# Where the residual of the second half joins, and which chunks carry no late row, in a hybrid attention and PEER block

## The chip, the cores and the metric

The kernel runs on one core of a Trainium2 chip. The metric is the device time of one execution in microseconds (us). Engines: PE (TensorE), ACT (ScalarE), DVE (VectorE), POOL (GpSimd), SP (SyncE, which here only issues DMAs). A core has 16 DMA engines, which all queues share.

## The reference, cut to what matters

The block mixes two attentions and then a PEER layer over 256 tokens of width 2048, all in fp32. Everything before the PEER layer is the same in both kernels. What the change touches is the end:

```python
    def chunk(args):                      # peer(): 128 experts for each token
        xi, ei, gi = args
        u = expert_down[ei]
        a = jax.nn.gelu(jnp.einsum('cd,ced->ce', xi, u)).astype(jnp.float32)
        w = (a * gi).astype(xi.dtype)
        return jnp.einsum('ce,ced->cd', w, expert_up[ei])
...
        x = x + peer(rms_norm(x, norm_ffn_gain[l]), ...)
    return rms_norm(x, norm_final_gain)
```

`expert_up` has 16384 rows of 2048 floats, 128 MB. Each token needs 128 of them.

## The kernel before

**Two ways to form the sum over experts.** The 256 tokens are two halves of 128. For half 0, and for the first 64 tokens of half 1, the weights of a token are spread into a dense row over all 16384 experts, and PE multiplies them with the whole table. The table is read in 128 chunks of 128 experts, 1024 KB each (`u_raw`, four buffers, issued by SP at L672; chunk i is requested once PE has finished chunk i-4). Half 0 accumulates in PSUM banks 4 to 7 ("a"), the 64 tokens of half 1 in banks 0 to 3 ("b").

For the last 64 tokens of half 1 there is no dense path. Each token sits in two partitions, so that 128 partitions times 64 slots hold its experts. POOL gathers one row per partition (`late_rows`, 1 MB a gather, L1375). First come 63 gathers of `expert_down`, each reduced on DVE to a column of dot products (`late_dot`), then 64 gathers of `expert_up`, which DVE multiplies by the weight and adds into `late_sum` (`late_add`, L2454 to L2459). These are 127 late operations. They use six buffers; a gather is requested when the operation that last used its buffer is done, and POOL issues its gathers in order. Buffer 4 lies where the weights of chunks 0 to 15 were, and buffer 5 where those of chunks 16 to 31 were, so their first gathers wait for those chunks.

**One chunk.** Seven of eight chunks are split in a high and a low part: ACT rounds `u_raw` to `u_hi` (L1835) and the weights to `c_hi` and `c_b`; DVE forms `c_lo` and the low half of `c_b` (`c_low`), then `u_lo` (L2439), and then does the late operation of that chunk; PE does 12 matmuls with `u_hi` and 8 with `u_lo`. Each eighth chunk (i % 8 = 7) is "whole": PE uses it in fp32 and DVE has only the late operation.

**Which chunk carries a late operation.**

```python
        late_chunks = [i for i in range(1, NKEYS) if i % LATE_SKIP]
...
            for n_, j in enumerate(range(len(late_chunks), LATE_OPS)):
                if n_ == FINAL_0_AFTER:
                    final_0()
                late_op(j)
            final_1()
```

With `LATE_SKIP` = 24, chunks 24, 48, 72, 96 and 120 carry none; 122 of the 127 operations lie beside a chunk, and five lie behind the last one: three, then `final_0` (the output of half 0 from PSUM), then two, of which the last is cut in four pieces of 512 columns.

**The end.** ACT copies banks 0 to 3 to `b_out` (L1894) and takes the sum of squares of half 0 (L1711) and its root (L1713). Behind the last chunk PE adds into each bank c, for half 1: the residual (a matmul with the identity, all 128 rows), the fold of `b_out` (rows 0 to 63), and, as each piece of `late_sum` is ready, its fold (rows 64 to 127). ACT and DVE then norm half 1 bank by bank (`final_stats_1`, `final_1`), and SP stores it. SP also requests `final_row`, the gain of the last norm, 1024 KB, right behind the request of chunk 124.

Of the kernel before, what the change touches and what calls it, by code (L numbers as in the profile page):

```python
# [24 lines left out]
ALU = mybir.AluOpType  # L25
# [3 lines left out]
P = 128  # L29
# [125 lines left out]
IDLE = 1  # L155
WHOLE = 8
POOL_FROM = 3
LATE_SKIP = 24
FINAL_0_AFTER = 3
PRE = 1  # L160
QUARTER = D // 4
BT = 4
# [1 line left out]
PAIRS = P // 2  # L164
# [9 lines left out]
def build(nc, x, norm_mix_gain, w_in, nsa_gate_bias, fox_forget_bias, merge_gate_bias, k_cmp_pos, k_cmp_w1,  # L174
          k_cmp_w2, v_cmp_pos, v_cmp_w1, v_cmp_w2, w_up_nsa, w_up_fox, w_out, norm_ffn_gain, peer_w_query,
          peer_sub_keys_1, peer_sub_keys_2, peer_expert_down, peer_expert_up, norm_final_gain, consts, out):
    with ExitStack() as ctx:
        def sem(name):
            return ctx.enter_context(nc.semaphore(name))
# [4 lines left out]
        def at(name, shape, kb, dt=F32):  # L184
            n = int(np.prod(shape[1:])) * 4
            assert base + kb * 1024 + n <= nc.sbuf_usable_end, name
            return nc.alloc_sbuf_tensor_at(name, shape, dt, offset=int(base + kb * 1024))
# [21 lines left out]
        def const(name, parts=P):  # L209
            lo, hi = CT[name]  # L210
            return ct[0:parts, lo:hi]

        ident = const("ident")
# [22 lines left out]
        xres = at("xres", [P, HALVES, D], 138)  # L236
# [66 lines left out]
        u_hi = at("u_hi", [P, 2, D], 178, F32R)  # L303
# [5 lines left out]
        late_sum = at("late_sum", [P, D], 90)  # L309
        b_out = at("b_out", [P, D], 98)  # L310
        pair_sum = at("pair_sum", [P, PAIRS], 8)
        late_rows = [at(f"late_rows{r}", [P, D], kb) for r, kb in enumerate(LATE_AT)]
# [43 lines left out]
        psum = ctx.enter_context(nc.psum_tensor("psum", [P, 8, 512], F32))  # L356
# [120 lines left out]
        u_hi_used = sem("u_hi_used")  # L477
# [4 lines left out]
        pair_ps = sem("pair_ps")  # L482
# [65 lines left out]
        for d in range(len(ring_slots) + PRE):  # L548
            r = order[d] if d < len(order) else ring[(d - len(order)) % RING]
            if d >= LAST_SIX:  # L550
                r = (1, 7, 6, 2, 0, 3)[(d - LAST_SIX) % 6]
# [4 lines left out]
        LATE_OPS = 2 * LATE - PRE  # L556
        late_chunks = [i for i in range(1, NKEYS) if i % LATE_SKIP]

# [4 lines left out]
        def last_down(r):  # L563

            return max([d for d in range(len(down_slot)) if down_slot[d] == r and r < 4], default=NG * GS - 1)
# [3 lines left out]
        for j in range(LATE_OPS):  # L569
            free = [r for r in range(len(LATE_AT)) if LATE_FREE[r] <= late_step(j)]  # L570
            r = min(free, key=lambda r: last_op.get(r, last_down(r) - NG * GS))
# [115 lines left out]
        def _(pe):  # L687
            def mm(*a, **k):
                return nc.tensor.matmul(*a, skip_group_check=True, **k)  # L689
# [486 lines left out]
            for b in range(NBX):  # L1176
# [6 lines left out]
                if b == XRES_AT:  # L1183
                    pe.wait_ge(numT_done, 2)
                    pe.wait_ge(wT_done, 2)
                    for c in range(4):
                        last = mm(psum[:, 4 + c, :], ident, xres[:, 0, 512 * c:512 * c + 512], start=True, stop=False)
# [13 lines left out]
            def col(c):  # L1201
                return slice(512 * c, 512 * c + 512)
# [5 lines left out]
                    last = mm(psum[:, 4 + c, :], c_lo[:, q % 2, :], u_hi[:, q % 2, col(c)], start=False, stop=False)  # L1208
                return last

            def high_b(q, first=False):

                both = c_b[:, q % 2].rearrange("p x t -> p (x t)")
                for c in range(4):
                    last = mm(psum[:, c, :], both, u_hi[:, q % 2, col(c)], start=first, stop=False)
                return last

            def low_a(q, r):

                for c in range(4):  # L1220
                    last = mm(psum[:, 4 + c, :], c_hi[:, q % 2, :], u_lo[r][:, col(c)], start=False, stop=False)
                return last

            def low_b(q, r):

                both = c_b[:, q % 2].rearrange("p x t -> p (x t)")
                for c in range(4):
                    last = mm(psum[:, c, :], both, u_lo[r][:, col(c)], start=False, stop=False)
                last.then_inc(chunk_used, 1)

            def split_up(m, q, r):

                pe.wait_ge(u_hi_done, m + 1)
                pe.wait_ge(c_lo_done, m + 2)
                high_a(q)
                high_b(q).then_inc(u_hi_used, 1)
                pe.wait_ge(u_lo_done, m + 1)
                low_a(q, r)
                low_b(q, r)
# [36 lines left out]
            pe.wait_ge(u_lo_done, 1)  # L1276
            low_a(0, 0)
            pe.wait_ge(W_out, NBX + NB1)
            pe.wait_ge(c_lo_done, 2)
            high_b(0, first=True).then_inc(u_hi_used, 1)  # L1280
            low_b(0, 0)
            sixteen(0, first=1)
            with pe.Fori(1, NKEYS // 16 - 1) as i:
# [7 lines left out]
            pe.wait_ge(tables_done, 2)  # L1291
            for c in range(4):
                pe.wait_ge(b_copied, c + 1)
                mm(psum[:, c, :], ident, xres[:, 1, col(c)], start=True, stop=False)
                mm(psum[0:PAIRS, c, :], pair_sum[:], b_out[:, col(c)], start=False, stop=True)
            for c in range(4):
                pe.wait_ge(late_used, LATE_OPS + c)
                mm(psum[PAIRS:P, c, :], pair_sum[:], late_sum[:, col(c)], start=False, stop=True).then_inc(pair_ps, 1)


        @block.gpsimd
# [134 lines left out]
        def _(act):  # L1436
# [278 lines left out]
            def final_stats_1():  # L1715
                i = 2 * HALVES + 1
                for c in range(4):
                    cs = slice(512 * c, 512 * c + 512)
                    act.wait_ge(pair_ps, c + 1)
                    A(xn[:, 1, cs], psum[:, c, :], ACT.Square, accum_out=ss_end[:, c:c + 1]).then_inc(part_sums, 1)  # L1720
                act.wait_ge(ms_done, 2)
                A(rms[:, i:i + 1], ss[:, i:i + 1], ACT.Sqrt, bias=eps[:, 0:1], scale=1.0 / D).then_inc(squares, 1)
                act.wait_ge(x2_done, 1)
                A(xn[:, 1, OUT_COLS[0]], xres[:, 1, OUT_COLS[0]], ACT.Copy, scale=rstd[:, i:i + 1]).then_inc(x2_done, 1)
# [168 lines left out]
            for c in range(4):  # L1893
                nc.scalar.copy(b_out[:, 512 * c:512 * c + 512], psum[:, c, :]).then_inc(b_copied, 1)  # L1894
            final_stats_0()
            final_stats_1()


        @block.vector
        def _(dve):  # L1900
            V = nc.vector
            tt, ts, stt = V.tensor_tensor, V.tensor_scalar, V.scalar_tensor_tensor
# [543 lines left out]
            def late_add(j):  # L2446
                r, slot = late_slot[j], DENSE[1] + j - (LATE - PRE)
                w = gw[1].rearrange("p h s -> p (h s)")[:, slot:slot + 1]
                dve.wait_ge(late_in[r], 16 * late_turn[j])
                dve.wait_ge(late_used, j)  # L2450
                if j == LATE_OPS - 1:
                    for c in range(4):
                        cs = slice(512 * c, 512 * c + 512)
                        stt(late_sum[:, cs], late_rows[r][:, cs], w, late_sum[:, cs], ALU.mult, ALU.add).then_inc(late_used, 1)  # L2454
                    return
                if j == LATE - PRE:
                    ins = ts(late_sum[:], late_rows[r][:], w, None, ALU.mult)
                else:
                    ins = stt(late_sum[:], late_rows[r][:], w, late_sum[:], ALU.mult, ALU.add)  # L2459
                ins.then_inc(late_used, 1)  # L2460
# [35 lines left out]
            def late_op(j):  # L2496
                if j < LATE - PRE:
                    late_dot(j)
                else:
                    late_add(j)  # L2500
                if j == LATE_A - PRE:
                    late_inner(0, LATE_A)
                if j == LATE_A - PRE + 3:
                    late_weights(1, 0, LATE_A)
                if j == LATE - PRE:
                    late_inner(LATE_A, LATE)
                if j == LATE - PRE + 3:
                    late_weights(2, LATE_A, LATE)

            def final_0():  # L2510
                i = 2 * HALVES
                dve.wait_ge(squares, 3)
                seq(V.reciprocal(rstd[:, i:i + 1], rms[:, i:i + 1]))
                settle()
                dve.wait_ge(row_loaded, 16)
                x2 = psum[:, 4:8, :].rearrange("p k n -> p (k n)")
                for cs in OUT_COLS:
                    stt(xn[:, 0, cs], x2[:, cs], rstd[:, i:i + 1], final_row[:, cs], ALU.mult, ALU.mult).then_inc(y_done, 1)
# [93 lines left out]
# [3 lines that stand above are left out]
# [28 lines left out]
```

## Time and profile before

| what | value |
|---|---|
| median of three runs | 1964.7 us (1962.78 to 1968.36) |
| the profiled execution, its own time | 1965.54 us |
| its span, first to last instruction | 1963.7 us |
| mean granted PE clock | 0.975 of full |
| busy share PE, DVE, ACT, POOL | 93%, 76%, 44%, 30% |
| the stretch with the chunks | about 1316 to 1945 us |

A row of the timeline gives the start in us from the span's start, the duration in us, engine, line, operation, output<-inputs, and in brackets how long the engine idled before it and what ended that. PE matmuls are in fp32 or, with `u_hi` and `u_lo`, in a rounded form that needs one pass; one fp32 matmul shows as two. "DMA" in the column of an issue is the time from request to landing.

### The profile page before, as it was taken

The numbers are of one execution on the slowest core, as the hardware profiler recorded it, in microseconds if no ns is written. First come the engines' busy times: TensorE is split into PE (matmuls) and PEld (weight loads), VectorE is DVE, ScalarE is ACT, GpSimd is POOL, SyncE is SP. The second block draws the span as 40 slices with busy tenths as digits, with TensorE's granted clock in tenths as the row PEclk, the third lists the DMA queues.
The fourth block names the chain that finished last, engine by engine and source line by source line (L and its number), as shares of the span: only waits on it lengthen the run. The fifth ranks groups of instructions, "written<-read, shape, count | busy, mean of one in ns | idle before, by whom it ended". The sixth has DMA issues, their size and how long they took to land.

```text
span 1963.7 us, 26424 instructions
## 1 busy us (share of the span) xinstructions
PE 1824.8 (93%) x10535; PEld 1507.1 (77%) x10535; DVE 1500.9 (76%) x2000; ACT 858.6 (44%) x1262; POOL 584.5 (30%) x371
## 2 busy tenths in 40 slices
PE   8999999999999999879989757679999999999997
PEld 7979987888899879878888735467767776777674
DVE  5454447544455457899999999979989898998888
ACT  4343336444433343223333278974444434443443
POOL 1302300000000002646567678742333122222422
PEclk9999999999999999989999988989999999999999
DMA  7864550465556645899999999979999999999995
GB/s 259 291 228 148 174 169 22 129 192 186 187 183 225 237 140 171 338 426 402 401 426 426 420 382 425 404 317 398 427 427 427 427 427 427 428 428 427 426 427 230
DMA packets 142676, 620.25 MB, mean 316 GB/s; under 512 B 9680, under 2 KB 20192, under 8 KB 84464
## 3 DMA queue, kind: packets, MB, share of 16 engines
q0 software_dynamic: 46352, 336.11, 41.2%
q1 hardware_dynamic: 93712, 280.05, 38.3%
q10 hardware_dynamic: 2512, 2.75, 0.4%
q8 instruction: 64, 1.05, 0.2%
q14 instruction: 36, 0.29, 0.0%
HBM read 616.77 MB, written 2.10 MB: 315 GB/s over the span
## 4 chain that ended last, share of the span: by engine, by line
PE 58%; DVE 19%; DMA 9%; ACT 7%; issue 6%; POOL 1%; DVEq 0%; ACTq 0%; POOLq 0%
PE psum L689 57%; DMA u_raw<-in_peer_expert_up_dram 8%; DVE down_rows L2310 7%; DVE late_sum L2459 2%; ACT oh L1779 1%; ACT oh L1766 1%; ACT oh L1764 1%; DMA late_rows<-in_peer_expert_down_dram,eidx 1%; DVE w_lo L1950 1%; DMA down_rows<-in_peer_expert_down_dram,eidx 1%; DVE u_lo L2439 1%; DVE late_rows L2310 1%; ACT w_hi L1472 1%; ACT u_hi L1835 1%; DVE onehot L2266 1%
## 5 line engine op out<-in xcount | busy, mean ns | idle before, releaser
L1950 DVE TENSOR_TENSOR w_lo<-raw,w_hi 128x2048 fp32r<-128x2048 f32 x124 | 291.5, 2350 | 334.2 <-ACT w_hi L1472 334.1
L1472 ACT CAST w_hi<-raw 128x2048 fp32r<-128x2048 f32 x124 | 236.4, 1907 | 400.2 <-PE psum L689 400.2
L689 PE MATMUL psum<-act_both,w_hi 128*128 128x256 f32 (+1 forms) x1664 | 389.0, 319 | 4.4 <-DVE w_lo L1950 4.4
L1835 ACT CAST u_hi<-u_raw 128x2048 fp32r<-128x2048 f32 x112 | 214.3, 1913 | 356.2 <-DMA u_raw<-in_peer_expert_up_dram 351.9
L1375 POOL DMA_INDIRECT down_rows<-in_peer_expert_down_dram,eidx x155 | 280.8, 1812 | 121.1 <-issue 44.7
L689 PE MATMUL psum<-act_both,w_lo 128*128 128x256 f32 x1088 | 305.7, 281 | 0.0
L689 PEld LDWEIGHTS psum<-act_both,w_hi 128*128 128x128 f32 x1664 | 277.4, 192 | 28.0 <-issue 3.0
L2439 DVE TENSOR_TENSOR u_lo<-u_raw,u_hi 128x2048 fp32r<-128x2048 f32 x112 | 256.7, 2292 | 0.0
L689 PEld LDWEIGHTS psum<-act_both,w_lo 128*128 128x128 f32 x1088 | 207.7, 191 | 0.0
L2310 DVE CUSTOM_DVE_ANT_0 down_rows<-down_rows,xn 128x2048 f32<-128x2048 f32 x91 | 205.5, 2288 | 0.9 <-DVE ind L2221 0.4
L689 PE MATMUL psum<-w_hi,act_both 128*128 128x512 f32 x640 | 202.1, 394 | 0.2 <-DVE w_lo L1950 0.2
L689 PE MATMUL psum<-u_hi,c_hi 128*128 128x512 f32 x448 | 185.2, 413 | 9.7 <-DVE c_b L2468 6.7
L689 PE MATMUL psum<-xT,rT 128*128 128x128 f32 x1216 | 167.4, 288 | 25.0 <-DVE dots L2338 17.8
L689 PEld LDWEIGHTS psum<-xT,rT 128*128 128x128 f32 x1216 | 153.7, 199 | 33.7 <-issue 16.8
L689 PE MATMUL psum<-u_hi,c_lo 128*128 128x512 f32 x448 | 176.3, 393 | 0.0
L1800 ACT COPY rT<-psum 128x512 f32<-128x512 f32 x152 | 85.6, 588 | 200.1 <-PE psum L1055 200.1
L1375 POOL DMA_INDIRECT late_rows<-in_peer_expert_up_dram,eidx x64 | 92.3, 1442 | 242.8 <-DVE late_sum L2459 212.5
L1372 POOL TENSOR_TENSOR xn<-xn,ffn_row 128x2048 f32<-128x2048 f32 x2 | 11.3, 5654 | 496.2 <-PE psum L707 496.2
L2310 DVE CUSTOM_DVE_ANT_0 late_rows<-late_rows,xn 128x2048 f32<-128x2048 f32 x63 | 143.6, 2286 | 9.0 <-DMA late_rows<-in_peer_expert_down_dram,eidx 8.8
L1375 POOL DMA_INDIRECT late_rows<-in_peer_expert_down_dram,eidx x63 | 85.5, 1357 | 217.4 <-DVE keep L2310 178.7
L2459 DVE SCALAR_TENSOR_TENSOR late_sum<-late_rows,gw,late_sum 128x2048 f32<-128x2048 f32 x62 | 145.5, 2347 | 1.2
L2310 DVE CUSTOM_DVE_ANT_0 down_rows<-down_rows,x_b 128x2048 f32<-128x2048 f32 x64 | 142.7, 2289 | 0.1
(342 smaller groups left out, 3175.7 us busy)
## 6 DMA issues: line engine op xcount, KB each, us to landing
u_raw<-in_peer_expert_up_dram SPq DMA_DIRECT2D x128, 1024.0 KB, 11.8
raw<-in_w_in_dram SPq DMA_DIRECT2D x76, 1024.0 KB, 5.0
raw<-in_w_out_dram SPq DMA_DIRECT2D x16, 1024.0 KB, 4.9
raw<-in_peer_w_query_dram SPq DMA_DIRECT2D x16, 1024.0 KB, 5.0
raw<-in_w_up_nsa_dram SPq DMA_DIRECT2D x8, 1024.0 KB, 5.0
raw<-in_w_up_fox_dram SPq DMA_DIRECT2D x8, 1024.0 KB, 5.0
cmp_w<-in_k_cmp_w_dram SPq DMA_DIRECT2D x4, 1024.0 KB, 10.7
cmp_w<-in_v_cmp_w_dram SPq DMA_DIRECT2D x4, 1024.0 KB, 10.6
```

The source lines that it names most:

```text
L689: return nc.tensor.matmul(*a, skip_group_check=True, **k)
L1375: nc.gpsimd.indirect_dma_start(rows[:], None, table, bass.IndirectOffsetOnAxis(ap=eidx[:, half, slot:slot + 1], axis=0)).then_inc(landed, 16)
L1472: nc.scalar.copy(w_hi[:, p % 2], raw[:, p]).then_inc(hi_done, 1)
L1764: A(both, psum[:, 0:2, :], ACT.Abs).then_inc(dist_done, 1)
L1766: A(both, both, ACT.Relu, bias=1.0, scale=-1.0).then_inc(rows_done, 1)
L1779: ins = A(oh[:, 1, par, q, :], oh[:, 1, par, q, :], ACT.Copy, scale=w[:, q:q + 1])
L1800: nc.scalar.copy(dst.rearrange("p k t -> p (k t)"), psum[:, r % 2, :]).then_inc(rT_done, 1)
L1835: nc.scalar.copy(u_hi[:, m % 2, :], u_raw[i % 4][:]).then_inc(u_hi_done, 1)
L1950: tt(w_lo[:, p % 2], raw[:, p], f32(w_hi[:, p % 2]), ALU.subtract).then_inc(lo_done, 1)
L2310: return V.tensor_tensor_reduce(out=rows[:], in0=rows[:], in1=x_, scale=1.0, scalar=0.0, op0=ALU.mult, op1=ALU.add, accum_out=out)
L2439: tt(u_lo[i % 4][:], u_raw[i % 4][:], f32(u_hi[:, m % 2, :]), ALU.subtract).then_inc(u_lo_done, 1)
L2459: ins = stt(late_sum[:], late_rows[r][:], w, late_sum[:], ALU.mult, ALU.add)
```

## The change

Four edits. (1) The residual of tokens 0 to 63 of half 1 goes into banks 0 to 3 at chunk 0: four matmuls with 64 rows of the identity, ahead of the first use of those banks, and the four residual matmuls behind the last chunk go away. (2) The residual of tokens 64 to 127 goes into `late_sum` with the first weighted row: an operation over 128 partitions becomes two over 64 each. (3) `LATE_SKIP` 24 becomes 32: chunks 32, 64 and 96 carry no late operation, 124 of 127 lie beside a chunk and, counted in the code, three instead of five behind the last one. (4) `FINAL_0_AFTER` 3 becomes 2: two of the three come before `final_0`, the cut one behind it. In the final matmuls, rows 0 to 63 and 64 to 127 each get a start of their own, and the count that ACT waits for is shifted by four.

```diff
-LATE_SKIP = 24
-FINAL_0_AFTER = 3
+LATE_SKIP = 32
+FINAL_0_AFTER = 2
...
             low_a(0, 0)
             pe.wait_ge(W_out, NBX + NB1)
+            for c in range(4):
+                mm(psum[:, c, :], ident[0:PAIRS, :], xres[0:PAIRS, 1, col(c)], start=True, stop=False)
             pe.wait_ge(c_lo_done, 2)
-            high_b(0, first=True).then_inc(u_hi_used, 1)
+            high_b(0).then_inc(u_hi_used, 1)
...
             for c in range(4):
                 pe.wait_ge(b_copied, c + 1)
-                mm(psum[:, c, :], ident, xres[:, 1, col(c)], start=True, stop=False)
-                mm(psum[0:PAIRS, c, :], pair_sum[:], b_out[:, col(c)], start=False, stop=True)
+                mm(psum[0:PAIRS, c, :], pair_sum[:], b_out[:, col(c)], start=True, stop=True).then_inc(pair_ps, 1)
             for c in range(4):
                 pe.wait_ge(late_used, LATE_OPS + c)
-                mm(psum[PAIRS:P, c, :], pair_sum[:], late_sum[:, col(c)], start=False, stop=True).then_inc(pair_ps, 1)
+                mm(psum[PAIRS:P, c, :], pair_sum[:], late_sum[:, col(c)], start=True, stop=True).then_inc(pair_ps, 1)
...
-                    act.wait_ge(pair_ps, c + 1)
+                    act.wait_ge(pair_ps, 4 + c + 1)
...
                 if j == LATE - PRE:
-                    ins = ts(late_sum[:], late_rows[r][:], w, None, ALU.mult)
+                    ts(late_sum[0:PAIRS], late_rows[r][0:PAIRS], w[0:PAIRS], None, ALU.mult)
+                    ins = stt(late_sum[PAIRS:P], late_rows[r][PAIRS:P], w[PAIRS:P], xres[PAIRS:P, 1, :], ALU.mult, ALU.add)
```

## Rows read from the trace of the kernel before

**Rows 1.** The page, busy time of each engine

```profile
PE 1824.8 (93%) x10535; PEld 1507.1 (77%) x10535; DVE 1500.9 (76%) x2000; ACT 858.6 (44%) x1262; POOL 584.5 (30%) x371
```

**Rows 2.** Busy time by stretch: PE, PEld, DVE, ACT, POOL, clock, DMA share, GB/s

```profile
1314.00:1322.00 8.00, 7.98 (x46) 6.71 (x45) 6.14 (x12) 6.39 (x9) 1.75 (x2) 1.00 0.01 2
1324.00:1342.00 18.00, 18.00 (x79) 14.45 (x78) 18.00 (x21) 9.32 (x14) 3.84 (x4) 1.00 0.93 350
1342.00:1900.00 558.00, 552.21 (x2232) 397.17 (x2231) 510.18 (x479) 228.40 (x328) 154.03 (x113) 1.00 1.01 427
```

**Rows 3.** The chain that ended last, 1900 us to the end

```profile
1909.98 15.32 DMA u_raw<-in_peer_expert_up_dram
...
1952.87 3.66 PE psum L689 x8
...
1958.33 1.15 ACT xn L1724
```

**Rows 4.** Timeline of ACT, chunks 122 to 125

```profile
1907.19 1.92 ACT L1835 CAST u_hi<-u_raw 128x2048 fp32r<-128x2048 f32 x1 [2.66 <-DMA u_raw<-in_peer_expert_up_dram]
...
1912.09 1.92 ACT L1835 CAST u_hi<-u_raw 128x2048 fp32r<-128x2048 f32 x1 [2.64 <-DMA u_raw<-in_peer_expert_up_dram]
...
1915.16 1.92 ACT L1835 CAST u_hi<-u_raw 128x2048 fp32r<-128x2048 f32 x1 [0.82 <-DMA u_raw<-in_peer_expert_up_dram]
...
1925.33 1.90 ACT L1835 CAST u_hi<-u_raw 128x2048 fp32r<-128x2048 f32 x1 [7.91 <-DMA u_raw<-in_peer_expert_up_dram]
```

**Rows 5.** Timeline of POOL, the gathers' requests around chunks 120 and 121

```profile
1898.32 0.94 POOL L1375 DMA_INDIRECT late_rows<-in_peer_expert_up_dram,eidx  x1 [0.30 <-issue]
1909.72 0.99 POOL L1375 DMA_INDIRECT late_rows<-in_peer_expert_up_dram,eidx  x1 [10.47 <-DVE late_sum L2459]
```

**Rows 6.** DMA requests in 1904 to 1907 us: size, us to landing

```profile
final_row<-in_norm_final_gain_dram SPq DMA_DIRECT2D x1, 1024.0 KB, 14.1
```

**Rows 7.** Timeline of POOL, the gathers around the first use of buffer 5

```profile
1443.95 0.98 POOL L1375 DMA_INDIRECT late_rows<-in_peer_expert_down_dram,eidx  x1 [4.01 <-DVE keep L2310]
1459.77 2.24 POOL L1375 DMA_INDIRECT late_rows<-in_peer_expert_down_dram,eidx  x1 [14.84 <-DVE c_b L2468]
```

**Rows 8.** The same two gathers, in order: us from request to landing

```profile
late_rows<-in_peer_expert_down_dram,eidx POOLq DMA_INDIRECT x1, 18.0
...
late_rows<-in_peer_expert_down_dram,eidx POOLq DMA_INDIRECT x1, 9.1
```

**Rows 9.** Timeline of SP from the request of chunk 4 on

```profile
1321.66 23.40 SPq L672 DMA_DIRECT2D u_raw<-in_peer_expert_up_dram  x6
```

**Rows 10.** Timeline of PE: the four residual matmuls of half 0, and what follows

```profile
1261.56 3.60 PE L689 MATMUL psum<-xres,ct 128*128 128x512 f32 x8
1265.00 1.05 PE L689 MATMUL psum<-oh 128*128 128x128 f32 x8
```

**Rows 11.** Timeline of DVE behind the last split chunk

```profile
1934.95 12.17 DVE L2459 SCALAR_TENSOR_TENSOR late_sum<-late_rows,gw,late_sum 128x2048 f32<-128x2048 f32 x5
1947.03 0.16 DVE L2513 RECIPROCAL keep<-keep 128x1 f32<-128x1 f32 x1
...
1949.62 2.34 DVE L2459 SCALAR_TENSOR_TENSOR late_sum<-late_rows,gw,late_sum 128x2048 f32<-128x2048 f32 x1
1952.07 2.74 DVE L2454 SCALAR_TENSOR_TENSOR late_sum<-late_rows,gw,late_sum 128x512 f32<-128x512 f32 x4
```

**Rows 12.** Timeline of ACT: the root of half 0

```profile
1946.63 0.29 ACT L1713 ACTIVATE keep<-keep 128x1 f32<-128x1 f32 x1
```

**Rows 13.** Timeline of PE: residual and fold behind the last chunk, first and last

```profile
1944.43 1.02 PE L689 MATMUL psum<-xres,ct 128*128 128x512 f32 x2
...
1951.56 1.07 PE L689 MATMUL psum<-b_out,pair_sum 128*64 128x512 f32 x2
```

**Rows 14.** Busy time by stretch around chunk 125, columns as in Rows 2

```profile
1928.00:1930.00 2.00, 1.83 (x6) 1.47 (x7) 2.00 (x2) 1.01 (x1) 0.00 (x0) 0.71 0.97 410
1930.00:1932.00 2.00, 2.00 (x6) 1.53 (x5) 2.00 (x2) 1.98 (x6) 0.00 (x0) 0.50 0.59 246
1932.00:1934.00 2.00, 2.00 (x10) 1.67 (x9) 2.00 (x4) 1.08 (x2) 1.24 (x1) 0.94 0.06 25
```

**Rows 15.** Timeline of DVE: the first weighted late row

```profile
1636.29 1.28 DVE L2457 TENSOR_SCALAR late_sum<-late_rows,gw 128x2048 f32<-128x2048 f32 x1
```

More of the change, by code:

```diff
@@ L1209, in high_a, with high_b @@
                 return last
-            def high_b(q, first=False):
+            def high_b(q):
                 both = c_b[:, q % 2].rearrange("p x t -> p (x t)")
                 for c in range(4):
-                    last = mm(psum[:, c, :], both, u_hi[:, q % 2, col(c)], start=first, stop=False)
+                    last = mm(psum[:, c, :], both, u_hi[:, q % 2, col(c)], start=False, stop=False)
                 return last
```

## The prediction, as put on record before the run

> **What bounds the kernel now.** The page comes first. PE is busy for 93% of the span and DVE for 76% [rows 1], which seems to make PE the bound. The table by stretch corrects that for the part that the change touches: from 1342 to 1900 us the DMA engines move 427 GB/s in the mean, at a share of 1.01, beside PE at 552 of 558 us and DVE at 510 [rows 2]. So I ask which of them the others wait for. In the timeline of ACT, which takes each chunk first, every cast of a chunk was released by its DMA, and the casts of chunks 122 and 123 lie 4.90 us apart [rows 4]. In 4.90 us 427 GB/s are 2.09 MB, that is, one chunk and one gather of 1.05 MB each. The stretch is paced by bytes, and one row set or chunk costs 2.45 us of the DMA engines. Last comes the chain from 1900 us on: it goes through the transfer of chunk 125, then DVE (late rows, `final_0`, late rows), then the last folds on PE and the norm [rows 3]. At the end, then, two clocks stand behind each other: bytes until chunk 125 lands at 1925.3, and DVE from there to the last late row.
>
> **The late rows that move into the loop.** Two of 127 late operations go from behind the last chunk to beside chunks (five behind become three). Their gathers, 1 MB each, were requested at the very end before; a gather needs the buffer of the sixth operation ahead of it, so at the end all gathers are requested two chunks earlier than before. Nothing is loaded more or less. But what lands ahead of chunk 125 is now up to two gathers more, and the loop has no free bytes. Bounds: nothing (if the gathers found free transfer time) and 2 x 2.45 = 4.9 us.
>
> To place it between, I look for stretches in which the gathers' queue was empty and the chunks had the DMA engines alone, for those are what an extra gather fills. There are two. The first hangs on the skip at chunk 120: gathers were requested at 1898.32 and then only at 1909.72, after POOL had waited 10.47 us for DVE [rows 5]. Chunk 124 then came 3.07 us after chunk 123 instead of 4.90 [rows 4], so the chunks gained 1.83 us. (Chunk 125 came 10.17 us later only because `final_row`, another 1024 KB, stands ahead of it in SP's queue [rows 6]; that stays.) With the skip gone, a gather is requested there too and the 1.83 us are lost. The second hangs on the skip at 24: the first gather into buffer 5 had to wait for the weights of chunk 31. The gather before it was requested at 1443.95 and landed 18.0 us later, at 1461.95; it was requested at 1459.77 and landed 9.1 us later, at 1468.87 [rows 7, 8]. That is 6.92 us between two landings, against 4.90 where both queues are full, so 2.02 us went to chunks. After the change buffer 5 is first used one operation later, and the gather ahead of it goes into buffer 4 without that wait, so the queue does not run dry. Together 1.83 + 2.02 = 3.85 us by which chunk 125 lands later. I take 3.8, below the 4.9. The skips at 48 and 72 gave the chunks nothing, since gathers were queued throughout; they only let the gathers run further ahead.
>
> The trace shows the two queues taking turns: one chunk and one gather per 4.90 us. The Trainium skill, page "DMA: Bandwidth & Descriptors", section "Queues, rings and completion order", says that each DMA engine goes round the queues that have work, a packet at a time. By that rule a late row in the loop is never free for the chunks, and this part would cost the full 4.9 us; by the idle stretches of the trace it is 3.8.
>
> **The tail behind chunk 125.** DVE adds late rows at 12.17 / 5 = 2.43 us each with the way between them, and 2.45 in the last case (1949.62 to 1952.07) [rows 11]. Before, three of them stand between the last chunk and `final_0`, and two behind it. `final_0` needs the root of half 0, which ACT starts at 1946.63 and ends at 1946.92 [rows 12]; DVE is there at 1947.03 [rows 11], so the two meet within 0.1 us. With one late row fewer ahead of it, DVE comes 2.4 us early and waits for ACT, which waits for PE's last chunk: that row gives nothing. The other, behind `final_0`, gives its full 2.45 us: the four pieces start where the whole row started, at 1949.62 counted from the same landing of chunk 125, instead of 1952.07. What could take it back is PE: residual and fold ran from 1944.43 to 1952.63, and the first fold of `late_sum` began at 1952.87 [rows 3, 13]. With the residual there, PE would have been next in line. Four residual matmuls out take about half of the 8.20 us away, so PE is free at about 1948.5 against a first piece at 1950.4. From the folds of `late_sum` on, nothing changes. So this part gives 2.45 us. Bounds: at least 2.1, as chunk 126 now comes a full 4.90 us after 125 and may cost DVE 0.3; at most 4.15, see the clock below.
>
> **The residual at chunk 0.** Four fp32 matmuls of 512 columns, as for half 0, where they held PE from 1261.56 to 1265.00, 3.44 us [rows 10]. Those are over 128 rows, the new ones over 64; no row here shows 64. I take 3.4, since they are issued alike. The Trainium skill, page "TensorE: Matmul & The Clock Gate", section "Why this matters for your kernels", says that a matmul over fewer rows alone takes the time of a full one; if the cost went with rows instead, it would be 1.7 us, and the sum about 0.8 us lower.
>
> Chunk 0 ends 3.4 us later, and its end releases the request of chunk 4, at 1321.66 before [rows 9]. That is a bad place: from 1314 to 1322 the DMA engines move next to nothing, 2 GB/s [rows 2], as all buffers are full, and the delay prolongs this. Bounds: 3.4 us, if every later request slides along, and 0. Between: from 1324 to 1342 the engines reach only 350 of 427 GB/s, which is 18 x (1 - 350/427) = 3.2 us of gaps [rows 2]. The gathers' requests slide less than the chunks' (the first late operation does not wait for the added matmuls), so the two queues overlap more and some gaps close. By 1342 both queues are full, and from then on bytes count. I take 1.5 us, nearly the middle.
>
> **The rest, at nothing.** The first weighted row was one operation of 1.28 us [rows 15]; now it is that and one like the others, 2.4 us more on DVE, once. Its cover: DVE has 558 - 510 = 48 us free in the loop [rows 2], 2.4 of it at each whole chunk, and the chunk requests have about two chunks outstanding. Without the cover it costs 2.4 us. The added count of `pair_ps` has no operation of its own.
>
> **The sum.** 3.8 + 1.5 - 2.45 = +2.85 us on the profiled execution's 1965.54 (span 1963.7), so about 1968.4 (span 1966.6). The median shown is 0.84 lower, 1964.7; plus 2.85 it is 1967.5.
>
> **Rivals.**
> - *Both delays in full, and the kernel is slower by more than 0.3% (5.9 us).* The head slides by 3.4 us with no gap closed, and the two gathers cost 4.9: 3.4 + 4.9 - 2.1 = +6.2, 1970.9. It decides once head and gathers together exceed 8.0 us. For it: the DMA engines are full for 558 us, so nothing later makes up a lost us. Against: the gaps before 1342 and the two dry stretches.
> - *The two late rows are hidden.* If gathers find time beside chunks, for example because PE, at 552 of 558 us, and not bytes is the clock, chunk 125 does not move: 0 + 0 to 1.5 - 2.45 gives 1962.3 to 1963.8. For it: PE's busy share. Against: ACT's waits for DMA.
> - *The clock of the tail.* PE idled before chunk 125 and then had 0.71, 0.50 and 0.94 of its clock in three stretches of 2 us [rows 14], which is 2 x (0.29 + 0.50 + 0.06) = 1.7 us lost. PE and the root of half 0 are what `final_0` would wait for after the change. If this drop falls elsewhere, the tail gives 2.45 + 1.7 = 4.15 and the sum is +1.2, 1965.9. If it grows by as much, +4.6, 1969.3.
> - *Faster by more than 0.3%* would need both moved rows to count in full (4.9), the better clock and no cost at all; I see no mechanism for more than 4.15 us.
>
> **How the numbers follow.** A measurement of this kernel tells about 0.3%, 5.9 us, from no change. Forecast: 0.57. Hidden rows: 0.18. The clock: 0.10. Both delays in full: 0.11. Something unseen, faster: 0.04. The first three lie within 0.3%, with small parts of the first beyond it: faster 0.05, same 0.82, slower 0.13. The range reaches down to the hidden rows (1962.3) and up to the full delays (1970.9), a little cut at neither end: 1962.0 to 1971.0.
>
> **What would show it.** Chunk 124 comes 4.90 us after 123, not 3.07; POOL has no wait of 10 us between its last gathers. Chunk 125's cast starts at 1930 to 1931 instead of 1925.33. DVE stands idle about 2.4 us before the reciprocal of `final_0`, released by ACT. The span from that cast to the end shrinks by 2.4 us. The request of chunk 4 lies 3.4 us later than at 1321.66, and chunk 8 or later only 1 to 2 us later. The prediction is wrong if chunk 125 lands where it did, if the idle stretch before chunk 4 is made up or carried in full, or if DVE does not wait before `final_0`.

## The result, and the profile after

The changed kernel has a median of 1971.84 us over 12 runs (1968.85 to 1975.96); the kernel before, 12 runs beside it, 1966.77 us. The ratio is 1.0024, with a 95% interval of 1.0015 to 1.0033, that is +4.7 us (3.0 to 6.5), computed on 1966.8. The ratio lies within 0.3%, as forecast, but the cost is above the +2.85 us forecast, and the median lies above the top of the range, 1971.0. Two things make that miss: the kernel before itself ran 2.1 us above the 1964.7 that the forecast stood on, and the change cost about 1.9 us more than the sum said (2.2 by the two medians).

ACT's timeline of the changed kernel, chunks 123 to 125:

```profile
1918.49 1.91 ACT L1836 CAST u_hi<-u_raw 128x2048 fp32r<-128x2048 f32 x1 [2.63 <-DMA u_raw<-in_peer_expert_up_dram]
...
1923.41 1.92 ACT L1836 CAST u_hi<-u_raw 128x2048 fp32r<-128x2048 f32 x1 [2.67 <-DMA u_raw<-in_peer_expert_up_dram]
...
1934.14 1.90 ACT L1836 CAST u_hi<-u_raw 128x2048 fp32r<-128x2048 f32 x1 [8.47 <-DMA u_raw<-in_peer_expert_up_dram]
```

Chunk 124 now comes 4.92 us after 123, where it came 3.07 us after it in [rows 4]. POOL's timeline shows the cause; the wait of 10.47 us [rows 5] is gone, 5.56 is the longest here:

```profile
1904.73 0.94 POOL L1376 DMA_INDIRECT late_rows<-in_peer_expert_up_dram,eidx  x1 [0.30 <-issue]
1911.23 0.97 POOL L1376 DMA_INDIRECT late_rows<-in_peer_expert_up_dram,eidx  x1 [5.56 <-DVE late_sum L2461]
```

DVE's timeline of the tail answers to [rows 11]:

```profile
1943.81 9.71 DVE L2461 SCALAR_TENSOR_TENSOR late_sum<-late_rows,gw,late_sum 128x2048 f32<-128x2048 f32 x4
1956.21 0.16 DVE L2515 RECIPROCAL keep<-keep 128x1 f32<-128x1 f32 x1 [2.68 <-ACT keep L1714]
...
1958.80 2.73 DVE L2455 SCALAR_TENSOR_TENSOR late_sum<-late_rows,gw,late_sum 128x512 f32<-128x512 f32 x4
```

Four late rows in a row instead of five, then DVE idles 2.68 us for the root of half 0, then `final_0`, then the four pieces at once. From the cast of chunk 125 to the pieces it was 1952.07 - 1925.33 = 26.74 us and is 1958.80 - 1934.14 = 24.66: 2.1 us less.

At the first use of buffer 5 [rows 7] POOL still waits as long as before, 14.73 us, but with one gather more requested ahead of it:

```profile
1450.12 0.94 POOL L1376 DMA_INDIRECT late_rows<-in_peer_expert_down_dram,eidx  x1 [4.00 <-DVE keep L2311]
1465.79 2.24 POOL L1376 DMA_INDIRECT late_rows<-in_peer_expert_down_dram,eidx  x1 [14.73 <-DVE c_b L2470]
```

At the head, the timelines of PE and SP:

```profile
1318.94 0.48 PE L689 MATMUL psum<-u_hi,c_hi 128*128 128x512 f32 x1
...
1321.89 3.70 PE L689 MATMUL psum<-xres,ct 64*128 64x512 f32 x8
1325.51 1.21 PE L689 MATMUL psum<-u_hi,c_b 128*128 128x512 f32 x4
```
```profile
1327.68 0.33 SPq L672 DMA_DIRECT2D u_raw<-in_peer_expert_up_dram  x1
```

Counted from the first matmul of chunk 0 (before 1316.82, after 1318.94), chunk 4 is requested after 8.74 us instead of 4.84. Chunk 0 starts 2.1 us later in this profile than in that of before; with the code ahead of it unchanged, it lies between 1314.1 and 1320.2 us in the thirteen profiles taken here. So I count every stage from that matmul.

Around chunk 125, PE's timeline and the table by stretch answer to [rows 13, 14]:

```profile
1936.99 0.77 PE L689 MATMUL psum<-u_hi,c_hi 128*128 128x512 f32 x1 [5.93 <-DVE c_b L2470]
...
1953.78 3.65 PE L689 MATMUL psum<-b_out,pair_sum 128*64 128x512 f32 x8
1959.60 3.65 PE L689 MATMUL psum<-late_sum,pair_sum 128*64 128x512 f32 x8 [2.17 <-DVE late_sum L2455]
```
```profile
1934.00:1936.00 2.00, 0.00 (x0) 0.00 (x0) 0.00 (x0) 1.85 (x2) 0.00 (x0) 0.62 1.03 434
1936.00:1938.00 2.00, 1.01 (x3) 0.84 (x4) 1.58 (x3) 0.39 (x3) 0.00 (x0) 0.50 0.99 418
1938.00:1940.00 2.00, 2.00 (x6) 1.62 (x5) 2.00 (x2) 1.01 (x1) 0.00 (x0) 0.50 0.93 389
1940.00:1942.00 2.00, 2.00 (x7) 1.57 (x7) 2.00 (x4) 1.98 (x6) 0.00 (x0) 0.67 0.19 78
```

PE idled 5.93 us, then began at half clock (0.50, that is 1.2 of 2.4 GHz) and had the whole clock back within 1940 to 1942 us. Behind the last chunk it now has only the folds of `b_out`, and then waits 2.17 us for `late_sum`.

### The profile page after: what moved, and what is told of

It is laid out like the page before. It is cut to its first block, busy times and chain, and to the rows that moved or that the text cites. A ratio compares the mean times of both kernels' runs of the same rounds, so it can differ in the third digit from the quotient of the medians.

```text
span 1970.5 us, 26424 instructions
## 1 busy us (share of the span) xinstructions
PE 1822.4 (92%) x10535; PEld 1508.2 (77%) x10535; DVE 1503.6 (76%) x2001; ACT 858.5 (44%) x1262; POOL 583.4 (30%) x371
## 4 chain that ended last, share of the span: by engine, by line
PE 59%; DVE 17%; DMA 11%; ACT 7%; issue 5%; POOL 1%; DVEq 0%; ACTq 0%
PE psum L689 57%; DMA u_raw<-in_peer_expert_up_dram 11%; DVE down_rows L2311 7%; ACT oh L1780 1%; ACT oh L1767 1%; ACT oh L1765 1%; DVE w_lo L1951 1%; ACT u_hi L1836 1%; DMA down_rows<-in_peer_expert_down_dram,eidx 1%; DVE late_sum L2461 1%; ACT w_hi L1473 1%; DVE onehot L2264 0%; DVE onehot L2267 0%; DVE key L2269 0%; PE psum L707 0%
## 5 line engine op out<-in xcount | busy, mean ns | idle before, releaser
L689 PE MATMUL psum<-xT,rT 128*128 128x128 f32 x1216 | 166.3, 287 | 26.7 <-DVE dots L2339 19.5
L1376 POOL DMA_INDIRECT late_rows<-in_peer_expert_up_dram,eidx x64 | 88.0, 1375 | 237.5 <-DVE late_sum L2461 200.0
```

The lines of the kernel that those rows point to most:

```text
L1376: nc.gpsimd.indirect_dma_start(rows[:], None, table, bass.IndirectOffsetOnAxis(ap=eidx[:, half, slot:slot + 1], axis=0)).then_inc(landed, 16)
```

## The experiments

Each ran 12 times (the residual twice, 7 times), with the kernel before beside it. The table puts together what they gave: the ratio and the same in us on 1966.8; from the timelines of ACT and DVE in one profile each, the cast of chunks 123 and 125 after chunk 0's first matmul, and the first of the four last pieces after the cast of chunk 125; and last, how much longer than before that profile is from chunk 0's first matmul to its end.

| kernel | ratio (95%) | us | cast 123 | cast 125 | pieces | chunk 0 to end |
|---|---|---|---|---|---|---|
| before | | 0 | 595.3 | 608.5 | 26.7 | 0 |
| changed | 1.0024 (1.0015 to 1.0033) | +4.7 | 599.5 | 615.2 | 24.7 | +4.7 |
| changed, again | 1.0017 (1.0008 to 1.0027) | +3.3 | 599.8 | 615.4 | 24.7 | +4.9 |
| residual edits only | 1.0025 (1.0016 to 1.0034) | +4.9 | 597.6 | 611.3 | 26.7 | +5.6 |
| skips only | 1.0010 (1.0001 to 1.0019) | +2.0 | 597.3 | 613.0 | 24.2 | +3.2 |
| residual at 125 | 1.0001 (0.9990 to 1.0011) | +0.2 | 597.5 | 613.1 | 25.5 | +3.3 |
| residual at 112 | 1.0007 (0.9999 to 1.0016) | +1.4 | 598.8 | 614.4 | 24.9 | +4.1 |
| `final_row` last | 0.9982 (0.9973 to 0.9992) | -3.5 | 595.6 | 604.8 | 27.2 | -3.2 |
| residual at 125, `final_row` last | 0.9990 (0.9980 to 0.9999) | -2.0 | 597.2 | 607.9 | 25.2 | -2.1 |
| residual twice | 1.0033 (1.0021 to 1.0045) | +6.5 | 603.5 | 619.2 | 24.5 | +8.5 |
| residual at 112, old skips | 1.0008 (0.9998 to 1.0018) | +1.6 | 595.6 | 608.9 | 27.7 | +3.1 |
| residual behind chunk 0 | 1.0024 (1.0012 to 1.0035) | +4.7 | 599.6 | 615.2 | 24.3 | +4.3 |
| residual at 112, `final_row` last | 0.9981 (0.9969 to 0.9993) | -3.7 | 598.1 | 608.8 | 23.0 | -1.7 |

The times and the last column agree in sign and roughly in order, but differ by up to 3 us. The times hold what lies ahead of chunk 0, where all these kernels have the same code; in the profile of "residual at 125" chunk 0 starts 2.8 us sooner than in that of before. A difference of 1 or 2 us between two kernels is therefore read from the profiles, behind that matmul.

**1. The residual edits alone.**

```diff
 # against the changed kernel
-LATE_SKIP = 32
-FINAL_0_AFTER = 2
+LATE_SKIP = 24
+FINAL_0_AFTER = 3
```

> The kernel before with the residual edits alone (chunk 0 and first weighted row); the skips stay at 24 and final_0 behind three late rows. Theory A, the head delay is carried in full: chunk 4 is requested 3.6 to 3.9 us later and chunk 125 lands 3.6 to 3.9 us later, both counted from the first matmul of chunk 0; DVE sets the tail as before, so nothing comes back: +3.8 us. Theory B, as in the prediction, gaps close: chunk 125 lands 1.5 us later, +1.5 us.

Measured: +4.9 us, as much as the whole change. Chunk 4 was requested 3.9 us late, as both theories had it. Chunk 125 came 2.8 us later than before (611.3 against 608.5), between the theories. The rest came from where neither looked, the tail: 2.8 us by the last column. PE's timeline and the table by stretch at its end:

```profile
1946.35 3.65 PE L689 MATMUL psum<-b_out,pair_sum 128*64 128x512 f32 x8
1954.86 6.43 PE L689 MATMUL psum<-late_sum,pair_sum 128*64 128x512 f32 x8 [4.86 <-DVE late_sum L2455]
```
```profile
1954.00:1956.00 2.00, 1.14 (x2) 0.52 (x3) 1.95 (x3) 0.00 (x0) 0.00 (x0) 0.50 0.00 0
1956.00:1958.00 2.00, 2.00 (x3) 0.46 (x2) 1.21 (x3) 0.69 (x2) 0.00 (x0) 0.50 0.00 0
```

With the residual matmuls gone, PE was through with `b_out` early, idled 4.86 us for the last late row, and its clock fell to 0.50. The last folds took 6.43 us instead of 3.65. The residual matmuls behind the last chunk had cost nothing, and they had kept PE at work. That the idle time alone made the clock fall is not shown; experiment 11 speaks against it.

**2. The skips alone.**

```diff
 # against the kernel before
-LATE_SKIP = 24
-FINAL_0_AFTER = 3
+LATE_SKIP = 32
+FINAL_0_AFTER = 2
```

> The kernel before with LATE_SKIP 32 and FINAL_0_AFTER 2 alone; the residual stays behind the last chunk. Theory A: only the chunks from 109 on come later, so that chunk 125 lands 2.9 us later (0.6 at chunk 109, 1.8 at chunk 124, 0.5 at 125), counted from the first matmul of chunk 0. Theory B: the wait for buffer 5 counts too and chunk 125 lands 3.8 us later or more. In both, residual and fold on PE now stand behind final_0's wait, so that the tail gives at most 0.3 us: +2.6 us by A, +3.5 us by B.

Measured: +2.0 us, and +3.2 by the last column. Chunk 125 came 4.5 us later, which is theory B, and the tail gave more than the 0.3 us expected: PE, with residual and fold still to do, ran into the late folds without a gap, and from the cast of chunk 125 to the end it took 1.3 us less than before. So the skips cost more at chunk 125 than they give behind it.

**3 and 4. The residual matmuls elsewhere.**

```diff
 # against the changed kernel; in the other run the loop stands ahead of "for j"
             for j in range(NKEYS - 16, NKEYS - 1):
+                if j == NKEYS - 3:
+                    for c in range(4):
+                        mm(psum[:, c, :], ident[0:PAIRS, :], xres[0:PAIRS, 1, col(c)], start=False, stop=False)
```

The first product in banks 0 to 3 at chunk 0 starts their sum, as in the kernel before.

> The changed kernel with the four residual matmuls moved from chunk 0 to right ahead of chunk 125, where PE idles for 5.9 us. Theory A, the place of these matmuls costs and not their work: chunk 4 is requested as before, chunk 125 lands 2.9 us later than in the kernel before, and the tail gives 2.0 to 4 us back, the more if PE keeps its clock: between -1 and +1 us against the kernel before, 4 to 6 us faster than the changed one. Theory B: the head delay counts for only 1.5 us, so this is 1.5 to 2 us faster than the changed kernel.

> The same, but the four matmuls stand ahead of chunk 112, in the middle of the stretch that is paced by bytes. Theory A: PE has about 0.3 us spare per chunk and the requests have two chunks outstanding, so 3.4 us of PE work there cost nothing: chunk 125 lands 2.9 us later than before, the tail gives 2.0 back: +0.9 us against the kernel before, about 3.8 us faster than the changed one. Rival: PE work delays the requests wherever it stands, and the time is that of the changed kernel, +4.7 us.

Measured: +0.2 and +1.4 us, where the changed kernel has +4.7 and +3.3 in its two sets of runs. The profiles grant less: by the last column the two are 1.3 to 1.6 and 0.6 to 0.8 us faster than the changed kernel, not about 4. What the matmuls themselves cost ahead of chunk 112 can be read locally, from ACT's timeline of experiment 4, the casts of chunks 110 and 122:

```profile
1850.68 1.92 ACT L1836 CAST u_hi<-u_raw 128x2048 fp32r<-128x2048 f32 x1 [2.67 <-DMA u_raw<-in_peer_expert_up_dram]
...
1910.39 1.92 ACT L1836 CAST u_hi<-u_raw 128x2048 fp32r<-128x2048 f32 x1 [2.63 <-DMA u_raw<-in_peer_expert_up_dram]
```

They lie 59.7 us apart. In nine of the ten profiles without the residual there it is 58.9, in that of experiment 1 59.0; in experiments 8 and 11, with the residual there, 59.8 and 59.2. So 3.4 us of PE work in the loop delay the chunks by 0.3 to 0.9 us, and at its head by about 2.2 (chunk 125 at 615.2 to 615.4 against 613.0 and 613.1). The rival of the fourth run, the same cost wherever it stands, falls by this, though its total is close. The clock was not held: in both, it was at half for 6.8 us from 1929.2 and 1931.8 us on.

**5. The request of `final_row` behind chunk 127.**

```diff
-                if i == NKEYS - 4:
+                if i == NKEYS - 1:
                     sp.dma_start(final_row[:], norm_final_gain.unsqueeze(0).partition_broadcast(P)).then_inc(row_loaded, 16)
```

> The kernel before with one request moved: final_row (1024 KB, needed only by final_0) is requested behind chunk 127 instead of behind chunk 124. Theory A, the landing of chunk 125 starts the tail: its cast comes 4.9 us sooner after that of chunk 124 than before, DVE reaches its first operation for chunk 125 about 3.5 us sooner (it is then bound by the late row of chunk 124), and the kernel is 3.5 us faster. Theory B, bytes are conserved and something else of the same size takes the place: no change.

Measured: -3.5 us (-1.6 to -5.3), -3.2 by the last column: theory A, though the match to the tenth is luck. ACT's and DVE's timelines:

```profile
1917.18 1.91 ACT L1835 CAST u_hi<-u_raw 128x2048 fp32r<-128x2048 f32 x1 [2.04 <-DMA u_raw<-in_peer_expert_up_dram]
...
1922.08 1.91 ACT L1835 CAST u_hi<-u_raw 128x2048 fp32r<-128x2048 f32 x1 [2.64 <-DMA u_raw<-in_peer_expert_up_dram]
```
```profile
1922.60 2.34 DVE L2459 SCALAR_TENSOR_TENSOR late_sum<-late_rows,gw,late_sum 128x2048 f32<-128x2048 f32 x1
1924.86 0.28 DVE L2464 TENSOR_TENSOR c_lo<-W_a,c_hi 128x128 fp32r<-128x128 f32 x1
```

Chunk 125 is cast 4.90 us after chunk 124 instead of 10.17 (chunk 124 came 1.5 us later, so the gain is 3.8 us), and DVE goes from the late row of chunk 124 straight to chunk 125, without the gap that it had.

**6. Experiments 3 and 5 together.**

> The changed kernel with the residual matmuls ahead of chunk 125 and final_row requested last. Theory A: what the extra late rows cost at chunk 125 (2.4 us) is covered by the 4.9 us that final_row gives, DVE has two late rows fewer behind it, and PE idles less ahead of chunk 125 and keeps its clock: 4 to 6 us faster than the kernel before. Theory B: DVE is then behind anyway and only one late row counts: 2.5 to 3.5 us faster.

Measured: -2.0 us, less than both theories, though the interval reaches to -3.9. DVE's timeline shows 3.23 us of idle time at `final_0`:

```profile
1933.61 9.71 DVE L2462 SCALAR_TENSOR_TENSOR late_sum<-late_rows,gw,late_sum 128x2048 f32<-128x2048 f32 x4
1946.55 0.16 DVE L2516 RECIPROCAL keep<-keep 128x1 f32<-128x1 f32 x1 [3.23 <-ACT keep L1715]
```

With chunk 125 early, PE has no idle time ahead of it to put the residual in.

**7. The residual twice at chunk 0.** The residual of tokens 0 to 63 of half 1 is added two times.

```diff
             for c in range(4):
                 mm(psum[:, c, :], ident[0:PAIRS, :], xres[0:PAIRS, 1, col(c)], start=True, stop=False)
+            for c in range(4):
+                mm(psum[:, c, :], ident[0:PAIRS, :], xres[0:PAIRS, 1, col(c)], start=False, stop=False)
```

> The changed kernel with the four residual matmuls at chunk 0 done twice (the residual of these 64 tokens is added two times). Theory A, the head delay is carried in full: chunk 4 is requested 3.4 us later still and the time is 3 to 3.5 us above that of the changed kernel, about +8 us against the kernel before. Theory B, only a part of a delay at this place is carried: 1 to 1.5 us above the changed kernel.

Measured: +6.5 us, 1.8 above the first set of the changed kernel and 3.1 above the second, so the times do not decide. The trace does: chunk 125 came 4.0 us later than in the changed kernel. The second 3.4 us are carried in full, and the last column, 3.5 to 3.8 us above the changed kernel, says the same.

**8. The residual edits with the old skips, without the head delay.**

```diff
 # against experiment 4
-LATE_SKIP = 32
-FINAL_0_AFTER = 2
+LATE_SKIP = 24
+FINAL_0_AFTER = 3
```

> Residual edits alone, as in the earlier run with the skips at 24, but with the four matmuls ahead of chunk 112, so without the head delay. Theory A: of the 4.9 us that the residual edits cost alone, the head took about 2.5 and the tail the rest, since PE waits longer for the last late row, its clock falls and the last folds take 2.8 us more: +2 to +3 us against the kernel before, with the clock at half in the last folds. Theory B: the head took all of it and the fall of the clock is chance: 0 us.

Measured: +1.6 us (-0.4 to +3.5). Chunk 125 is where it was (608.9), and the time from its cast to the end is 2.7 us longer: the pieces start 0.9 us later after it, and the last folds, with the clock at half from 1955.5 us on, take 5.34 us instead of 3.65. The loss in the tail of experiment 1 comes back without the head.

**9 and 10. The residual right behind chunk 0, and the changed kernel again.**

```diff
 # against the changed kernel
-            for c in range(4):
-                mm(psum[:, c, :], ident[0:PAIRS, :], xres[0:PAIRS, 1, col(c)], start=True, stop=False)
...
-            high_b(0).then_inc(u_hi_used, 1)
+            high_b(0, first=True).then_inc(u_hi_used, 1)
             low_b(0, 0)
+            for c in range(4):
+                mm(psum[:, c, :], ident[0:PAIRS, :], xres[0:PAIRS, 1, col(c)], start=False, stop=False)
```

> The changed kernel with the four residual matmuls right behind chunk 0's last use instead of ahead of its second half, so that the request of chunk 4 and the high part of chunk 2 are no longer held up, while the request of chunk 5 and all later ones are. Theory A, the cost hangs on the stretch in which the DMA engines stand still until chunk 4 is requested: chunk 4 is requested 4.8 us after the first matmul of chunk 0, as before, and the kernel is 2 to 3 us faster than the changed one. Theory B, any 3.4 us of PE work in the first chunks costs the same, as the DMA queues are short there: the time of the changed kernel, within 1 us.

> The changed kernel once more, unaltered, as the neighbour of the run above and for a second profile. In the trace: chunk 4 requested 8.7 us after the first matmul of chunk 0, the cast of chunk 125 at 614 to 616 us after it, and 36.3 us from there to the end, within about 1 us each; +4 to +5.5 us against the kernel before. If the cast of chunk 125 lies outside 614 to 616, one profile is no ground for terms of 1 us.

Measured: +4.7 us, and +3.3 for its neighbour, the changed kernel. Chunk 4 was requested 4.8 us after the first matmul, as in the kernel before, and chunk 125 still came at 615.2. My theory A falls: the cost does not hang on the request of chunk 4. The table by stretch for the 28 us behind chunk 0's start, then the 62 behind those, of this kernel, of the changed one and of the one before:

```profile
1315.00:1343.00 28.00, 28.00 (x119) 21.38 (x118) 25.34 (x26) 14.55 (x22) 3.85 (x4) 1.00 0.68 252
1343.00:1405.00 62.00, 62.00 (x259) 46.02 (x258) 57.97 (x61) 24.64 (x34) 22.36 (x14) 1.00 1.01 418
```
```profile
1319.00:1347.00 28.00, 28.00 (x117) 21.29 (x116) 24.17 (x26) 14.39 (x22) 3.83 (x4) 1.00 0.66 252
1347.00:1409.00 62.00, 62.00 (x258) 46.10 (x257) 59.03 (x61) 25.22 (x37) 22.86 (x15) 1.00 1.01 425
```
```profile
1317.00:1345.00 28.00, 28.00 (x122) 22.38 (x121) 26.14 (x30) 14.60 (x22) 4.36 (x5) 1.00 0.75 281
1345.00:1407.00 62.00, 62.00 (x257) 45.75 (x256) 58.37 (x60) 26.06 (x36) 19.89 (x15) 1.00 1.01 427
```

In the first 28 us the DMA engines move 281 GB/s before and 252 after, 29 x 28 / 427 = 1.9 us of their time lost, wherever in chunk 0 or behind it the matmuls stand. Counted from the first matmul, all eight kernels without added matmuls there move 278 to 283 GB/s, the four with them 250 to 257, and experiment 7, with twice as many, 220. PE is busy for all 28 us in all three tables. In the first chunks it is PE that sets the pace of the requests; the DMA queues are not yet full.

The second profile of the changed kernel has chunk 125 at 615.4 and 24.7 us from there to the pieces, against 615.2 and 24.7, so at chunk 125 and behind it terms of 1 us can be read. Between chunk 8 and chunk 108 they can't: experiment 5, whose code there is that of before, has its casts up to 1.7 us later and at chunk 122 only 0.3. Ahead of chunk 0, single profiles scatter by some us.

**11. Experiments 4 and 5 together.**

> The changed kernel with the residual matmuls ahead of chunk 112 and final_row requested last. In the run that had them ahead of chunk 125, PE was busy without a gap from there on, and DVE waited 3.2 us for the root of half 0. Theory A: those 3.6 us of PE work were on the path; ahead of chunk 112 they are not, DVE waits at most 0.5 us at final_0, and the kernel is 4.5 to 5.5 us faster than before, the fastest of all. Theory B: the bytes of the two late rows ahead of chunk 125 set the end, and it is like the kernel that only requests final_row last, 3 to 4 us faster than before.

Measured: -3.7 us (-1.4 to -6.1): theory B's size, not told apart from experiment 5 by the times; by the last column it gains 1.5 us less. DVE waits 0.98 us at `final_0`, and the pieces start 3.8 us sooner after chunk 125 than before. But the clock fell again, to half from 1948.4 us on, in the last folds, and from the first piece to the end of the folds it took 6.1 us instead of 4.5:

```profile
1948.05 5.34 PE L689 MATMUL psum<-late_sum,pair_sum 128*64 128x512 f32 x8 [2.18 <-DVE late_sum L2455]
```

PE had idled 2.18 us ahead of them, as long as in the changed kernel (2.17), which kept its clock. Experiments 5 and 11 are the fastest kernels; the one with a single moved request is the simpler.

## Why the prediction was right or wrong

**Right: the clocks.** The chunks are paced by bytes, the tail by DVE, and moving the two rows costs more at the first than it gives at the second. Chunk 124 came 4.92 us after 123, the missing wait on POOL, the idle DVE at `final_0` (2.68 us, 2.4 forecast) and the early chunks' request (3.9 us later) were all seen. The sign was right, and so was a cost within 0.3%.

**Wrong: three sizes, all on the same side.**

- *The late rows ahead of chunk 125*, taken at 3.8 us, "below the 4.9". Kernels with the old skips have chunk 125 at 608.5 and 608.9, those with the new ones at 613.0, 613.1 and 614.4; with the residual at chunk 0, 611.3 against 615.2, 615.4 and 615.2. That is 4.8 and 4.0 us, 4.4 in the mean. The term of 1.83 us at chunk 124 measured 4.92 - 3.07 = 1.85. The prediction let the 10.17 us between chunks 124 and 125 stay; they became 10.73, so 0.6 us more came there that the sum had at nothing. The term of 2.02 us, put down to buffer 5, has its size in the end (at chunk 123 the new skips are 1.6 to 3.2 us late, like with like). Its place is shown in part: from the cast of chunk 30 to that of chunk 33 the four kernels with the old skips take 9.2 to 10.3 us, the nine with the new ones 11.7 to 14.7, and three full turns are 14.7. But single kernels differ by up to 2 us at chunk 20, where none of this code has run yet, so it can't be priced there.
- *The residual at chunk 0*, taken at 1.5 us, "nearly the middle". Chunk 125 came 2.6 us later with it under the old skips (611.3 against 608.7) and 2.2 under the new, where no residual stood ahead of chunk 125; its doubling 4.0 more. The times (3.1 to 4.5 us against experiment 3, 3.3 between experiments 1 and 8) give more, but hold the scatter ahead of chunk 0. So it is 2.2 to 2.6 us. The mechanism was half right: DMA time is lost at the head, but not because chunk 4's request is late; behind chunk 0 the matmuls cost the same. Nor do the gaps close by 1342: in experiment 1 the chunks are 4.0 us late from chunk 36 to 96 and 2.3 at chunk 122. Why 1.7 us come back only there stays open.
- *The tail*, taken at 2.45 us, gave 2.1. The clock is why: PE idled 5.93 us ahead of chunk 125 and began it at 1936.99 at half clock, which ended at about 1941.3 (0.67 over 1940 to 1942 is half for 1.3 us and full for 0.7). So 4.3 us of its work ran at half, 2.15 us lost against 1.7 in [rows 14], and `final_0` came 0.4 us later after that cast. The other kernels with the new skips and `final_row` where it was bear this out: PE's work at half from there on was 3.3, 3.5, 3.9, 4.3, 4.4, 4.8 and 6.0 us (experiments 2, 9, 7, the changed kernel twice, 4 and 3), and the pieces came 24.2, 24.3, 24.5, 24.7, 24.7, 24.9 and 25.5 us after the cast, half a us for each us at half.

4.4 + 2.2 - 2.1 = +4.5 us, beside +4.7 and +3.3 measured in the two sets, and +4.7 and +4.9 in their profiles.

**The step that failed** is "some gaps close. By 1342 both queues are full, and from then on bytes count. I take 1.5 us, nearly the middle". It measured 2.2 us or more. With it goes the reading that the two dry stretches of the gathers' queue are the whole price of the late rows, 3.8 us: it left the stretch between chunks 124 and 125 at nothing, and the rows measured 4.4. In both I had the bound from bytes, 3.4 and 4.9 us, and went further below it than the traces allow. The third step is the tail, 2.45 us with the clock's loss as before; it gave 2.1. The rival "both delays in full", +6.2 us at a chance of 0.11, lies nearer to the measured +4.7 than the forecast does; the range above was cut to 1971.0 although that case alone reaches 1970.9 from a three-run median whose own runs went to 1968.36.

**Two rules of the Trainium skill.** The Trainium skill, "DMA: Bandwidth & Descriptors", section "Queues, rings and completion order", with its turns between queues, priced the two rows at 4.9 us; measured 4.4. The rule of the Trainium skill, "TensorE: Matmul & The Clock Gate", section "Why this matters for your kernels", that fewer rows alone save no time holds here: the four matmuls (eight passes) over 64 rows took 3.70 us, those over 128 rows 3.60 [rows 10].

## What to carry to other kernels

Where a stretch is paced by bytes, price what is moved into it, or ahead in a queue, at its bytes; and ask which transfer in front of the last needed one can wait, as 1 MB of gain row did here for 3.5 us with one line. Put filler work on PE where its queues are long: four matmuls of 3.4 us cost 2.2 to 2.6 us at the head of the loop and 0.3 to 0.9 us in its middle. Work that hides in a tail may be what holds PE's clock for the step behind it. And count stages from a common instruction: here whole times held up to 3 us that no edit had made.

## What the runs showed of the hardware that was not expected

Taking 4.1 us of matmuls out of PE's tail made its last eight matmuls slower, 6.43 us instead of 3.65, with the granted clock at 0.50, after 4.86 us of idle time. In the changed kernel PE idled 2.17 us at the same place and kept the clock; in experiment 11 it idled 2.18 us there, and the clock fell 0.4 us after it had begun again. So the idle time ahead of a step does not alone say at which clock it runs; what else does is not shown here.

DVE's timeline at the first weighted row of the changed kernel:

```profile
1642.05 1.27 DVE L2458 TENSOR_SCALAR late_sum<-late_rows,gw 64x2048 f32<-64x2048 f32 x1
1643.34 2.35 DVE L2459 SCALAR_TENSOR_TENSOR late_sum<-late_rows,gw,xres 64x2048 f32<-64x2048 f32 x1
```

Over 64 partitions the multiply took 1.27 us, over 128 it took 1.28 [rows 15]: half of the partitions saves nothing, and the split row cost DVE 2.3 us more, which shows nowhere at chunk 125.
